# Weight slabs rounded and subtracted in one 128x2048 operation instead of two of 128x1024

## The reference

```
u, v, z = jnp.split(h @ w_in, 3, axis=-1)          # sgu, mla: the same pattern
x = x + mixed @ w_out[l]
x = x + jnp.square(jax.nn.relu(h2 @ w_up[l])) @ w_down[l]
```

## Time and profile before

| | |
|---|---|
| runs of the kernel before | 2586.72, 2589.05, 2590.45 us; median 2589.05 |
| profiled execution, its span from first to last instruction | 2587.7 us; no other time is given for this execution |
| mean granted PE clock | 0.991 |
| PE, DVE, ACT, POOL busy | 98%, 63%, 53%, 16% of the span |
| rounding L437, 128x1024 | 838 times, 881.2 us |
| subtraction L1021, 128x1024 | 838 times, 1083.6 us |
| eviction L456 to stage, 128x512 | 156 times, 593 ns each |
| transfers | 549.06 MB, mean 212 GB/s |

### The profile page before, as it was taken

How to read it: one execution, slowest core, us unless ns; L and a number is a source line. 1 busy time by engine, 2 the same in 40 slices (tenths; PEclk the granted TensorE clock), 3 DMA queues, 4 the chain that set the end, 5 groups by cost and what they waited for, 6 DMA issues and landing times.

```text
span 2587.7 us, 33489 instructions
## 1 busy us (share of the span) xinstructions
PE 2523.5 (98%) x11958; PEld 2085.6 (81%) x11958; DVE 1635.7 (63%) x2516; ACT 1358.7 (53%) x1918; POOL 413.8 (16%) x288
## 2 busy tenths in 40 slices
PE   4999999999998999998999999999999999999999
PEld 3788788888887888887887788788888888888887
DVE  7779987767677677766655554555545545545544
ACT  4555664444447455555476666654544444444443
POOL 0155462111020000010000000034100011110111
PEclk8999999999999999999999999999999999999999
DMA  9989877778785766654545454555565555565554
GB/s 350 314 276 340 293 250 256 270 278 285 254 290 155 217 208 199 201 179 153 183 152 173 152 163 148 177 176 182 180 195 186 188 195 184 190 195 180 184 189 147
DMA packets 363831, 549.06 MB, mean 212 GB/s; under 512 B 32332, under 2 KB 126128, under 8 KB 363312
## 3 DMA queue, kind: packets, MB, share of 16 engines
q1 hardware_dynamic: 361872, 541.24, 63.3%
q10 hardware_dynamic: 1824, 6.04, 0.6%
HBM read 545.13 MB, written 2.10 MB: 211 GB/s over the span
## 4 chain that ended last, share of the span: by engine, by line
PE 92%; DVE 4%; issue 2%; ACT 2%; DMA 0%; SPq 0%; POOL 0%; ACTq 0%; DVEq 0%; POOLq 0%
PE ps L1943 54%; PE ps L1948 27%; PE ps L1928 1%; PE ps L1930 1%; PE ps L1929 1%; DVE ps L1050 1%; PE ps L2019 1%; DVE lo L1021 1%; PE ps L1968 1%; PE ps L2249 1%; PE ps L2248 1%; ACT hi L437 1%; PE ps L2123 1%; PE ps L2036 0%; PE ps L2040 0%
## 5 line engine op out<-in xcount | busy, mean ns | idle before, releaser
L1021 DVE TENSOR_TENSOR lo<-raw,hi 128x1024 fp32r<-128x1024 f32 x838 | 1083.6, 1304 | 747.5 <-ACT hi L437 746.7
L437 ACT ACTIVATE hi<-raw 128x1024 fp32r<-128x1024 f32 x838 | 881.2, 1058 | 763.7 <-PE ps L1948 677.0
L1943 PE MATMUL ps<-hi,a_hi 128*128 128x512 f32 (+1 forms) x2144 | 852.9, 398 | 6.8 <-issue 4.7
L1943 PE MATMUL ps<-hi,a_lo 128*128 128x512 f32 (+1 forms) x2144 | 838.1, 391 | 0.0
L1948 PE MATMUL ps<-lo,a_hi 128*128 128x512 f32 (+1 forms) x2144 | 575.2, 390 | 0.6 <-DVE lo L1021 0.6
L1943 PEld LDWEIGHTS ps<-hi,a_hi 128*128 128x128 f32 x2144 | 404.6, 189 | 95.5 <-issue 11.6
L1948 PEld LDWEIGHTS ps<-lo,a_hi 128*128 128x128 f32 x2144 | 403.4, 188 | 86.3 <-DVE lo L1021 1.5
L1943 PEld LDWEIGHTS ps<-hi,a_lo 128*128 128x128 f32 x2144 | 404.6, 189 | 79.6
L1943 PE MATMUL ps<-hi,b_hi 128*128 128x512 f32 x1024 | 404.1, 395 | 0.3 <-ACT y L769 0.3
L1943 PE MATMUL ps<-hi,b_lo 128*128 128x512 f32 x1024 | 399.3, 390 | 0.0
L1948 PE MATMUL ps<-lo,b_hi 128*128 128x512 f32 x1024 | 274.3, 390 | 0.0
(11 more groups left out here) (290 smaller groups left out, 1904.3 us busy)
## 6 DMA issues: line engine op xcount, KB each, us to landing
raw<-in_ada_w SPq DMA_DIRECT2D x96, 1024.0 KB
raw<-in_sgu_w_in SPq DMA_DIRECT2D x96, 1024.0 KB
raw<-in_w_up SPq DMA_DIRECT2D x64, 1024.0 KB
raw<-in_w_down SPq DMA_DIRECT2D x64, 1024.0 KB
raw<-in_w_in SPq DMA_DIRECT2D x42, 1024.0 KB
raw<-in_sgu_w_out SPq DMA_DIRECT2D x32, 1024.0 KB
raw<-in_w_in SPq DMA_DIRECT2D x128, 256.0 KB
raw<-in_mla_w_in SPq DMA_DIRECT2D x33, 512.0 KB
```

Source lines behind the costliest of these rows:

```text
L437: nc.scalar.activation(hi[:, q % CHUNKS, :], raw[:, r % RAWS, q % 2 * CW:(q % 2 + 1) * CW], ACT.Copy).then_inc(hi_ready, 1)
L1021: nc.vector.tensor_tensor(lo[:, q % CHUNKS, :], raw[:, r % RAWS, q % 2 * CW:(q % 2 + 1) * CW], hi[:, q % CHUNKS, :].bitcast(F32), ALU.subt ...
L1943: nc.tensor.matmul(ps[:, 2 * s + t, 0:width], x[:, k0 + j, t * P:(t + 1) * P], hi[:, c, w], start=begins, stop=False)
```

## The change

For every slab but the first, the two roundings become one of 128x2048, and so do the two subtractions. Both are done in the step of the odd chunk; they signal 2. In the step of an even chunk DVE does nothing, and ACT still waits for `chunk_used` as before, but no longer for the slab. The first slab (`SINGLES = 2` chunks) is treated in two parts as before.

```
+SINGLES = 2
 def hi_next(act, n, ahead=AHEAD):
     q = n.chunk.base + ahead
+    act.wait_ge(chunk_used, n.chunk.at(ahead + 1))
+    if q % 2 == 0 and q >= SINGLES:
+        return
+    wide = 1 if q < SINGLES else 2
     r = raw_of(q)
...
     act.wait_ge(landed[r % RAWS], here)
-    act.wait_ge(chunk_used, n.chunk.at(ahead + 1))
-    nc.scalar.activation(hi[:, q % CHUNKS, :], raw[:, r % RAWS, q % 2 * CW:(q % 2 + 1) * CW],
-                         ACT.Copy).then_inc(hi_ready, 1)
+    first = (q - wide + 1) % CHUNKS
+    nc.scalar.activation(hi[:, first:first + wide, :].rearrange("p a b -> p (a b)"),
+                         raw[:, r % RAWS, (q % 2 - wide + 1) * CW:(q % 2 + 1) * CW], ACT.Copy).then_inc(hi_ready, wide)
 def lo_next(dve, n, ahead=AHEAD):
     q = n.chunk.base + ahead
+    if q % 2 == 0 and q >= SINGLES:
+        return
+    wide = 1 if q < SINGLES else 2
     r = raw_of(q)
     dve.wait_ge(hi_ready, n.chunk.at(ahead + 1))
-    nc.vector.tensor_tensor(lo[:, q % CHUNKS, :], raw[:, r % RAWS, q % 2 * CW:(q % 2 + 1) * CW],
-                            hi[:, q % CHUNKS, :].bitcast(F32), ALU.subtract).then_inc(lo_ready, 1)
+    first = (q - wide + 1) % CHUNKS
+    flat = lambda a: a[:, first:first + wide, :].rearrange("p a b -> p (a b)")
+    nc.vector.tensor_tensor(flat(lo), raw[:, r % RAWS, (q % 2 - wide + 1) * CW:(q % 2 + 1) * CW],
+                            flat(hi).bitcast(F32), ALU.subtract).then_inc(lo_ready, wide)
     if q % 2:
         raw_done(dve, n)
```

## The result

| | before | after |
|---|---|---|
| runs | 2586.72 to 2590.45 us, median 2588.84 | 2706.70 to 2717.23 us, median 2713.98 |
| ratio, 95% interval | | 1.0484 [1.0469, 1.0499] |
| span of the profiled execution | 2587.7 us | 2715.4 us |
| mean granted PE clock | 0.991 | 0.977 |

A forecast was written before the change was run, and what follows sets the result against it. PE was taken to bound the kernel, busy 2523.5 of 2587.7 us. Span 2587.7 + 63 (mixed turns) + 8 (heads) + 8 (layer changes, opening) = 2667, or 2668 as run median; range 2608 to 2702.

The forecast's parts named there:

- Durations: Wide rounding on ACT 1.99 us, wide subtraction on DVE 2.29; work saved at most 0.1 us per slab and engine.
- Plain blocks at nothing: Plain matmul blocks, including the 894 us behind the mixed turns: wide operations covered, 5.5 us against 7.2, costing nothing.
- A mixed turn costs 7.8 us by waits: Linear attention beside window attention: first block 5.3 us late, second 2.5; eight turns, 63 us.
- mask to exponentials: Mixed turn, first block: mask and maximum start behind the wide subtraction, so PE gets the exponentials 0.4 us late.
- first copy: Mixed turn, first block: copy (L1679) behind the wide subtraction of chunks 4 and 5; PE waits 2.0 us for values.
- exponentials again: Mixed turn, half a block later: mask and exponentials behind wide work on chunks 6 and 7, another 1.2 us late.
- second copy: Mixed turn, end of first block: copy behind the wide subtraction of chunks 8 and 9, another 1.7 us late.
- masked copies: Mixed turn, second block: two masked copies (L1702) behind the subtraction of chunks 14 and 15; PE waits 1.7 us more.
- The clock as a rival: Mixed turns: one drop of granted PE clock to 0.50 per turn, 2.5 us each, 20 more, 2688; chance 0.12.
- Layer changes and opening at 8 us: Two layer changes and the opening, similar ACT and DVE chains: 4, 2 and 2 us, bounds -9 and 20.
- MLA heads 8 us: MLA heads, three groups of four: keys 1.0 us late, two more places 0.8 each; 8 us, bounds 0 and 16.
- Not slower, by the freed even step: ACT's even step no longer waits for its slab, removing PE idle and clock loss in the opening: 2580; chance 0.09.

The follow-up runs named there:

- narrow late operations: Against the changed kernel, roundings and subtractions narrow (128x1024), both of a slab still in the odd chunk's step, each signalling by itself: 2634.68 us (1.0182).
- the copies first: Against the changed kernel, in mixed turns DVE copies swa_pt and masks h_a one step earlier, ahead of the wide subtractions: 2651.63 us (1.0234).

## Why the prediction was wrong

- *Durations.* Right: 1.92 and 2.36 us in the mean against 1.99 and 2.29, 418 of each. The work saved was more than the "at most" of 0.1 us a slab and engine: ACT's roundings took 79 us less in all than in the earlier trace rows, DVE's subtractions 96, some 0.2 a slab. Beside PE it was worth nothing, as I said. By the prediction's own durations a slab is given back 2.0 us later (1.99 + 2.29 against 1.06 + 1.22), not 2.3; nothing hangs on it.
- *Plain blocks at nothing.* Right: 0.9 and 1.8 us in 1330, and shown alone.
- *A mixed turn costs 7.8 us by waits.* Right to 0.2: with the clock held up by filler work it was 8.0. The mechanism is right; that the sum is so close is in part luck, since terms too high and too low cancel. Term by term, in the turn shown: mask to exponentials 0.27 (forecast 0.4), first copy 1.70 (2.0), exponentials again none (1.2), second copy 2.16 (1.7), lo 0.29 (0.65), products none (0.2), masked copies 1.53 (1.7). The waits sum to 6.0. Of the 2 us missing to 8.0, 1.2 are hidden under the slow clock: with the clock full, the waits for exponentials (L2387) are 12.3 / 8 = 1.5 us a turn, 0.27 and 1.2, near the forecast. The other 0.8 the waits view doesn't show.
- *The clock as a rival, 2.5 us a turn with a chance of 0.12.* This is the step that failed most. I had a price, 20 us for eight turns, and the runs show 21, but that is luck: I had priced one drop of 5 us in each turn; there were 18 of 3.41, which halve the clock for 61 us and so cost 31, of which 9 were hidden. I had the sign: the row of 882 to 892, at 0.50, which starts in the last part of a wait of 3.0 us for DVE (L2248, ended at 882.29). But I argued "each wait is followed by full work at once", and treated as an alternative what comes on top of the waits. The sum should have been 2668 + 20.
- *Layer changes and opening at 8 us.* This term is the second step that failed, mis-sized: 30. I took them as "chains of the same kind" without following any. In the first change PE's waits rose from 7.6 to 19.3 us (summing its idle stretches), where 4 were forecast in all, and its clock fell from 0.98 to 0.92, 7 us more. In the second change the time at 0.50 rose from 6.8 to 10.2 us, which is 1.7 of its 5.0; the rest wasn't followed. The upper bound of 20 was the bound for all three and is exceeded by 10.
- *MLA heads 8 us.* Nearly right, 9.9. By PE's waits there, those for lo ahead of the keys (L1938) are new, 3.3 us in four, and those for y (L2275), 3.1 in four, none over 1.0; I had one place of 1.0 and two of 0.8 in each of three groups.
- *Not slower, by the freed even step.* This rival fell, as I thought: the copies missed their date, and putting the wait back changes little.

Against my sum that is 22 us more for the turns (21 of it the clock), 22 for the three stages, 2 for the heads and 3 for the plain blocks: 49, and the span is 48 longer than forecast (2715.4 against 2667).

The rule of the Trainium skill (Perfetto Trace Analysis, Optimizing Scalar/DVE Operations) held where it speaks against the change: breaking up operations of engines that aren't saturated lets work finish sooner, here 2634.68 against 2713.98 us for the same work at the same place in the queue. Its other side, that grouping helps a saturated engine, gained nothing in the opening, if 86% busy counts as saturated: with DVE busy for 255 of 296 us before it lost 7.4 us, where PE waits 5.4 us (3.5 before) for the small copies `wt` of DVE, and 3.3 us for hi, which it never did before.

## What to carry to other kernels

Merging two operations of a producer and two of a consumer on another engine saves 0.1 to 0.2 us of work on each engine here and costs the overlap, 0.9 us a pair; count the chain from the first start to the last end, not the engines' busy time. Then ask what small work is queued behind the long operation, and move it ahead. Where PE is at full clock and gets new waits like these of 1.7 and 2.2 us, add the slower clock to the sum as a term, and follow every stage that has such chains, not only the one with the most of them.

## What the runs showed of the hardware that was not expected

- In the turns, all 15 waits ahead of the values, 1.62 to 2.19 us long, were followed by 3.41 us at a granted clock of 0.50, and so were three of the eight waits of 1.53 to 1.55 us ahead of the states; the other five were not. Single waits up to 1.2 us, in the kernels with narrow late operations and with the wide subtraction alone, were followed by none.
- These runs show no sharp bound: a wait of 1.72 us for y at the end of the turns (L2365, at 1809.63) was followed by none, and the last turn with the copies first had waits of 1.50 and 1.05 us for exponentials and 1.73 for y, and kept 1.00.
- A third of what the slow clock costs in PE work (9 of 30 us) was hidden under waits that would have come anyway.
- A 128x2048 rounding took 1.92 us in the mean, and a 128x2048 copy with a scale 1.99.
